# The two middle column chunks of both output projections: four of eight quads as seven products instead of eight, and the residual turned in the last chunk

## The chip, the cores and the metric

One core of one Trainium2 chip runs the whole program. The time is the device's, in microseconds (us) for one execution. A span is the time from the first to the last instruction that the profiler recorded in one profiled execution.

## What is computed

A decoder trunk of two layers on 256 tokens of width 2048, in float32. Cut to what matters:

```
for layer in (0, 1):
    h = rmsnorm(x, ln_mix_g[layer])
    x = x + mixer(h)          # its last step: o (256 x 2048) @ w_o (2048 x 2048)
    h = rmsnorm(x, ln_mlp_g[layer])
    x = x + square(relu(h @ w_up)) @ w_down     # 2048 -> 8192 -> 2048
```

The mixer of layer 0 has eight stick-breaking and eight forgetting-attention heads, that of layer 1 is latent attention with sixteen heads. Both end in an output projection of the 16 heads' outputs, 128 columns each, with `w_o` (layer 0) and `mla_w_o` (layer 1).

## The kernel before, in words

**Precision.** A float32 operand is split into a rounded high half and a low half, and each product is three matmuls: high by high, high by low, low by high. The activations' halves lie in `h` (normed residual, turned so that the width is on the partitions) and `a` (attention outputs or feed-forward activations, turned too). The weights' halves are made while they stream through.

**Pieces.** All weights pass in one fixed order of *pieces*, numbered through the kernel. SyncE loads 512 rows by 512 columns (1 MB) into one of four `raw` slots; a slot makes two pieces of 128x1024. ScalarE rounds a piece to its high half (`split_hi`, L756, copy at L769), VectorE subtracts to get the low half (`split_lo`, L1075, L1078), TensorE multiplies. There are four pairs of halves, and `AHEAD` is 4: `split_hi(n + 4)` waits until TensorE has used piece n. TensorE's piece waits for `lo_done`, VectorE's split for `hi_done`. Each engine has one queue in program order. What else an engine does behind piece n stands in a plan (`plan_steps`, L225), a list of named steps for each piece; each engine's `mixer` function (ScalarE L976, VectorE L1321, TensorE L1764) walks over the pieces and does its part of the steps.

**An output projection** is four column chunks o0 to o3 of eight pieces each. A piece covers two 128-row tiles of w_o; with two token tiles it is 4 products of 3 matmuls of 128x512, 12 matmuls (`piece_rows`, L1534). Two PSUM banks hold a chunk's sum for the two token tiles. When a chunk is done VectorE adds it to the residual `x_tok` (L1332). Three pieces into the next chunk TensorE turns the four new 128-column tiles of the residual (`turn_x`, L1610, eight transposes by the identity), ScalarE takes the squares and the high halves (`turned_x`, L811), VectorE the low halves (`h_split`, L1093); this is done in o1, o2 and o3 for the chunk before, and for the last chunk behind the third piece of the feed-forward part. In o0 the last four heads of the attention are still being computed, among the pieces.

**The feed-forward part** is four blocks a layer. A block has four up chunks (`piece_cols`, L1583; 8 matmuls of 512 columns and 8 of 256 a piece), then chunk 0 of the down projection, then chunks 1 and 2 together as a *set*, then chunk 3. The set is cut along its rows into eight *quads* (two 128-row tiles by two column chunks by two token tiles: 2x2 blocks times 2x2 blocks). A plain quad (`plain_quad`, L1851) is two pieces and 8 products. A fast quad (`fast_quad`, L1835) has 7 products (Winograd's form), in four pieces:

- the raw piece of column chunk 1 (6 matmuls), as before;
- `t13` (6 matmuls), sums of neighbouring weight blocks that POOL's DMA makes (`u_load`, `u_add`, L669 to L691): two loads of 256 KB into a `u_sum` buffer, then two more that add onto it;
- `t24` (6 matmuls), two further sums by VectorE (`weight_sums`, L1382, additions at L1391 and L1393);
- `b22` (3 matmuls), one half-size piece of 128x512.

It needs sums of the activations too: VectorE makes four of 128x128 (`token_sums`, L1395 to L1407), ScalarE rounds them (`token_sums_hi`, L1020), VectorE makes their low half (`token_sums_lo`, L1409). Six of eight quads are fast there. Their token sums are made during the up chunks and chunk 0. Eight PSUM banks X1 to X8 collect the products; at the end ScalarE copies two of them (L1049) and VectorE joins the sums in twelve `combine` steps (L1417), the last four of them the additions to the residual.

**POOL's queue** has, in mixer 0, eight products for the forget gates (L659), each waiting for a head's scores; in mixer 1 rotary products and the halves of heads 16 to 29 (`split_out`, L710); and in both feed-forward parts the weight sums (L693).

Of the kernel before, what the change touches and what calls it, by code (L numbers as in the profile page):

```python
# [57 lines left out]

def plan_chunks():

    def full(matrix, col, width=N, k_tiles=KT):
        return [(matrix, 4, 4 * P * l, col, width) for l in range(k_tiles // 4)]
# [10 lines left out]
    for c in range(4):  # L73
        first.append((f"o{c}", "cols", full("w_o", c * N)))
# [6 lines left out]
    for c in range(4):  # L81
        second.append((f"o{c}", "cols", full("mla_w_o", c * N)))
    return first, second
# [4 lines left out]
PLAIN_QUADS = 2, 5  # L88
U_BUFFER = 0, 1, 2, 3, 0, 1
BLOCK_PIECES = 32 + 8 + 4 * len(FAST_QUADS) + 2 * len(PLAIN_QUADS) + 8  # L90


P_MIX0 = 0
P_MLP0 = 2 * sum(len(c[2]) for c in MIX0)
P_MIX1 = P_MLP0 + NB * BLOCK_PIECES
P_MLP1 = P_MIX1 + 2 * sum(len(c[2]) for c in MIX1)
P_END = P_MLP1 + NB * BLOCK_PIECES
L_MLP0 = P_MLP0 // 2
L_MIX1 = L_MLP0 + 32 * NB
L_MLP1 = L_MIX1 + (P_MLP1 - P_MIX1) // 2  # L100
# [10 lines left out]
def block_no(layer, b0):  # L111
    return NB * layer + b0
# [22 lines left out]
def summed_count(layer, b0, m):  # L135

    return 32 * (3 * block_no(layer, b0) + m // 2 + 1)


def stepped_count(layer, b0, m):  # L140
    return 2 * (6 * block_no(layer, b0) + m + 1)
# [6 lines left out]
def all_pieces():  # L148
    out, seen = {}, set()

    def put(n, kind, load, half, count=0):
        out[n] = (kind, load, half, kind in ("raw", "b22") and load not in seen, count)
        if kind in ("raw", "b22"):
            seen.add(load)
    for n in range(P_MIX0, P_MLP0):
        put(n, "raw", n // 2, n % 2)
    for n in range(P_MIX1, P_MLP1):
        put(n, "raw", L_MIX1 + (n - P_MIX1) // 2, n % 2)
    for layer in range(2):
        for b0 in range(NB):  # L160
            for i, (kind, load, half) in enumerate(block_plan(layer, b0)):
                count = {"t13": summed_count(layer, b0, load), "t24": stepped_count(layer, b0, load)}.get(kind, 0)
                put(block_base(layer, b0) + i, kind, load, half, count)
    return out
# [6 lines left out]
def pieces_of(chunks, start):  # L171

    out, n = {}, start
    for _, _, loads in chunks:
        for _, kts, _, _, width in loads:
            out[n] = out[n + 1] = (kts // 2, width)
            n += 2
# [10 lines left out]
def chunk_starts(chunks, start):  # L188
    out, n = {}, start
    for name, _, loads in chunks:  # L190
        out[name] = n
        n += 2 * len(loads)
    return out


AT0, AT1 = chunk_starts(MIX0, P_MIX0), chunk_starts(MIX1, P_MIX1)


ROWS0 = {c[0]: n for n, c in enumerate(x for x in MIX0 if x[1] != "cols")}
ROWS1 = {c[0]: n + len(ROWS0) for n, c in enumerate(x for x in MIX1 if x[1] != "cols")}  # L200
# [5 lines left out]
LAST_TURN_BANK = 0, 4, 6  # L206
GAIN_COL = (0, 32, 16, 48)
# [17 lines left out]
def plan_steps():  # L225
# [75 lines left out]
    at(o + 5, ("probs", 31), ("out", 30), ("out", 31))  # L301
    for at_, chunks in ((AT0, MIX0), (AT1, MIX1)):
# [13 lines left out]
    for n in [*range(P_MIX0, P_MLP0), *range(P_MIX1, P_MLP1)]:  # L316
        if n >= FIRST - 1 and not any(what == "split" for what, _ in plan.get(n, [])):
            plan.setdefault(n, []).insert(0, ("split", 0))
    plan[AT0["k2"]].sort(key=lambda step: ("probs", "split").index(step[0]))
# [13 lines left out]
def build(nc, x, positions, ln_mix_g, ln_mlp_g, sf_w_in, sf_b_f, fox_q_g, fox_k_g, sf_w_o,  # L333
# [4 lines left out]
    with ExitStack() as ctx:  # L338
# [7 lines left out]
        x_tok = sb("x_tok", [P, TT, D])  # L346
        h = sb("h", [P, KT, 2, T], F32R)
# [90 lines left out]

        def out_on_pool(n):

            return 16 <= n < 30
# [7 lines left out]
        X1, X2, X3, X4, X5, X6, X7, X8 = (psum[:, b] for b in (2, 6, 4, 7, 0, 5, 1, 3))  # L449
# [60 lines left out]
        def raw_piece(n):  # L510
# [5 lines left out]
            if kind[0] == "t":  # L516
                pair = u_sum[U_BUFFER[load]] if kind == "t13" else v_sum[load % 2]
# [107 lines left out]
        def _(pool):  # L625
# [28 lines left out]

            pool.wait_ge(cum_ready, 1)
            for n in range(NHG):
                if n >= 2:
                    pool.wait_ge(scores_done, NHG + n - 1)
# [1288 lines left out]
```

## Time and profile before

| | us |
|---|---|
| median of 3 runs | 2058.27 (2058.08 to 2058.28) |
| the profiled execution's own time | 2057.91 |
| its span | 2056.2 |
| TensorE busy (matmuls) | 2049.1 |
| VectorE busy | 1453.8 |
| ScalarE busy | 1109.3 |
| POOL busy | 217.2 |

PE is TensorE (PEld its weight loads), DVE VectorE, ACT ScalarE, POOL GpSimd, SP SyncE. Matmuls overlap, so the duration of one (389 ns) is more than the distance from one start to the next, and a full PE row is no statement about its speed. A row of the timeline is an instruction, or several of the same line one after the other: start in us, duration in us, engine, line, operation, what it writes and reads, shape, and in brackets how long the engine was idle ahead of it and who ended that.

### The profile page before, as it was taken

The page shows a single profiled execution, that of the slowest core. Times are in us where ns is not written, and L with a number is a line of the kernel's source. Part 1 is how long each engine was busy: PE and PEld are TensorE (multiplying, and loading weights), DVE is VectorE, ACT ScalarE, POOL GpSimd, SP SyncE. Part 2 cuts the span into 40 slices and gives each one's busy share as a digit, 9 for nine tenths or more (in the row PEclk, how much of TensorE's full clock was granted, in tenths as well). Part 3 has the DMA queues.
Part 4 walks back from the last instruction along what each step waited for, and adds up shares of the span by engine and source line. Part 5 has one row for each costly group of instructions (what it writes and reads, how often), then busy time and mean ns, then how long its engine had stood idle before and what let it go on. Part 6 is the DMA issues. An engine that isn't in the chain of part 4 may idle for free.

```text
span 2056.2 us, 26460 instructions
## 1 busy us (share of the span) xinstructions
PE 2049.1 (100%) x10488; PEld 1757.1 (85%) x10488; DVE 1453.8 (71%) x1967; ACT 1109.3 (54%) x1592; POOL 217.2 (11%) x317
## 2 busy tenths in 40 slices
PE   9999999999999999999999999999999999999999
PEld 8898888888888888888889888888888888888887
DVE  6556555566966877786696788557786696687777
ACT  6555565454644544554466786444554464454454
POOL 0000000020210120110010255001110021012010
PEclk9999999999999999999999999999999999999999
DMA  8555555585885795696576533568696588679565
GB/s 286 174 154 182 170 165 163 185 252 197 258 265 195 233 289 178 201 308 204 189 244 188 157 124 122 169 203 246 198 306 202 194 260 265 200 226 291 180 199 190
DMA packets 222195, 432.35 MB, mean 210 GB/s; under 512 B 12076, under 2 KB 26488, under 8 KB 222072
## 3 DMA queue, kind: packets, MB, share of 16 engines
q1 hardware_dynamic: 200520, 380.29, 55.6%
q0 software_dynamic: 21504, 50.34, 10.6%
q8 instruction: 84, 1.38, 0.3%
q14 instruction: 39, 0.32, 0.0%
q10 hardware_dynamic: 48, 0.02, 0.0%
HBM read 428.52 MB, written 2.10 MB: 209 GB/s over the span
## 4 chain that ended last, share of the span: by engine, by line
PE 98%; ACT 1%; DVE 1%; issue 0%; POOL 0%; POOLq 0%; DVEq 0%
PE psum L1592 23%; PE psum L1545 14%; PE psum L1547 14%; PE psum L1546 14%; PE psum L1595 12%; PE psum L1829 5%; PE psum L1828 5%; PE psum L1830 5%; PE psum L1674 1%; PE psum L1761 1%; PE psum L1616 1%; PE psum L1738 0%; PE psum L1762 0%; PE psum L1718 0%; PE psum L1719 0%; ACT nat L841 0%
## 5 line engine op out<-in xcount | busy, mean ns | idle before, releaser
L1078 DVE TENSOR_TENSOR halves<-raw,halves 128x1024 fp32r<-128x1024 f32 (+2 forms) x736 | 852.9, 1166 | 442.3 <-ACT halves L769 438.2
L769 ACT CAST halves<-raw 128x1024 fp32r<-128x1024 f32 (+2 forms) x736 | 728.3, 1001 | 593.3 <-PE psum L1547 298.6
L1592 PE MATMUL psum<-h,halves 128*128 128x512 f32 x2048 | 489.8, 391 | 0.0
L1592 PEld LDWEIGHTS psum<-h,halves 128*128 128x128 f32 x2048 | 376.4, 188 | 72.8
L1545 PE MATMUL psum<-halves,a 128*128 128x512 f32 x828 | 325.4, 393 | 0.3 <-ACT mix L836 0.3
L1547 PE MATMUL psum<-halves,a 128*128 128x512 f32 x828 | 322.6, 390 | 0.0
L1546 PE MATMUL psum<-halves,a 128*128 128x512 f32 x828 | 322.2, 389 | 0.0
L1595 PEld LDWEIGHTS psum<-h,halves 128*128 128x128 f32 x2048 | 262.7, 191 | 10.0
L1595 PE MATMUL psum<-h,halves 128*128 128x256 f32 x2048 | 266.1, 283 | 0.0
L1545 PE MATMUL psum<-halves,h 128*128 128x512 f32 (+4 forms) x572 | 213.4, 373 | 0.2 <-DVE h L1276 0.2
L1547 PE MATMUL psum<-halves,h 128*128 128x512 f32 (+4 forms) x572 | 206.9, 362 | 0.0
L1546 PE MATMUL psum<-halves,h 128*128 128x512 f32 (+4 forms) x572 | 206.5, 361 | 0.0
L1547 PEld LDWEIGHTS psum<-halves,a 128*128 128x128 f32 x828 | 155.4, 188 | 32.7
L1545 PEld LDWEIGHTS psum<-halves,a 128*128 128x128 f32 x828 | 155.5, 188 | 31.9 <-ACT mix L836 0.6
L1546 PEld LDWEIGHTS psum<-halves,a 128*128 128x128 f32 x828 | 155.6, 188 | 31.5
L682 POOL DMA_DIRECT2D mix<-in_mlp_w_down x48 | 29.5, 628 | 1193.3 <-DVE halves L1078 1117.2
L1547 PEld LDWEIGHTS psum<-halves,h 128*128 128x128 f32 x572 | 107.5, 188 | 15.4
L1545 PEld LDWEIGHTS psum<-halves,h 128*128 128x128 f32 x572 | 107.7, 188 | 14.5 <-issue 0.6
L1546 PEld LDWEIGHTS psum<-halves,h 128*128 128x128 f32 x572 | 107.8, 188 | 13.9
L1828 PE MATMUL psum<-halves,a 128*128 128x512 f32 x272 | 105.8, 389 | 0.0
L1829 PE MATMUL psum<-halves,a 128*128 128x512 f32 x272 | 105.8, 389 | 0.0
L1830 PE MATMUL psum<-halves,a 128*128 128x512 f32 x272 | 105.8, 389 | 0.0
(265 smaller groups left out, 2083.8 us busy)
## 6 DMA issues: line engine op xcount, KB each, us to landing
raw<-in_mlp_w_up SPq DMA_DIRECT2D x128, 1024.0 KB, 6.1
raw<-in_mlp_w_down SPq DMA_DIRECT2D x128, 1024.0 KB, 5.2
mix<-in_mlp_w_down POOLq DMA_DIRECT2D x192, 256.0 KB, 7.1
raw<-in_sf_w_in SPq DMA_DIRECT2D x41, 1024.0 KB, 5.2
raw<-in_sf_w_o SPq DMA_DIRECT2D x16, 1024.0 KB, 5.2
raw<-in_mla_w_o SPq DMA_DIRECT2D x16, 1024.0 KB, 5.1
raw<-in_mla_w_ukv SPq DMA_DIRECT2D x8, 1024.0 KB, 5.5
raw<-in_sf_w_in SPq DMA_DIRECT2D x14, 512.0 KB, 3.9
```

The costliest lines, as they stand in the source:

```text
L682: pool.dma_start(u[:, 0], b11).then_inc(u_loaded[m % 2], 16)
L769: nc.scalar.copy(half_piece(n, 0), raw_piece(n)).then_inc(hi_done, 1)
L1078: v.tensor_tensor(half_piece(n, 1), raw_piece(n), half_piece(n, 0).bitcast(F32), ALU.subtract)\
L1545: mm(bank, x_hi, hi[:, i], start=(k == 0), stop=False)
L1546: mm(bank, x_hi, lo[:, i], start=False, stop=False)
L1547: last = mm(bank, x_lo, hi[:, i], start=False, stop=(k == total_kts - 1))
L1592: last = mm(bank, half_piece(n, 0)[:, cols], src[:, k].rearrange("p s t -> p (s t)"), start=(k == 0), stop=(k == KT - 1))
L1595: last = mm(bank[:, T:2 * T], half_piece(n, 1)[:, cols], src[:, k, 0], start=False, stop=False)
L1616: ins = nc.tensor.transpose(psum[:, bank + i // 2, col:col + P], x_tok[:, tt, k * P:(k + 1) * P], ident[:])
L1828: mm(bank, x_hi, w_hi, start=start, stop=False)
L1829: mm(bank, x_hi, w_lo, start=False, stop=False)
L1830: return mm(bank, x_lo, w_hi, start=False, stop=stop)
```

## The change

Both output projections become o0, a *set* (chunks 1 and 2 together) and o3. In the set the quads 1, 3, 5, 7 are fast, in the form of the feed-forward set, and 0, 2, 4, 6 plain: 24 pieces in place of 16. The pieces of the set are numbered 0 to 23 here: quads at 0-1, 2-5, 6-7, 8-11, 12-13, 14-17, 18-19, 20-23. The loads of the two chunks alternate on SyncE's queue. The attention outputs exist only as halves in `a`, so VectorE first adds them (`out_y`), then makes the four sums. The steps of the plan: token sums behind the seventh piece of o0 and behind set pieces 1, 7, 13, their low halves one piece later; weight sums behind the seventh piece of o0 (ahead of the split there) and behind set pieces 3, 9, 15; the twelve combination steps from set piece 22 to the fifth piece of o3; the residual's three turns behind the fourth, sixth and eighth piece of o3. The first four pieces of the feed-forward part wait for two parts of `h`. POOL gets the loads and adds of four sums in each mixer. The halves of the token sums use parts of `h`, which is free then. The feed-forward blocks keep their form and only count their semaphores on.

```diff
+def output_chunks(matrix):
+    pairs = [load for both in zip(full(matrix, N), full(matrix, 2 * N)) for load in both]
+    return [("o0", "cols", full(matrix, 0)), ("set", "set", pairs), ("o3", "cols", full(matrix, 3 * N))]
...
+OUT_FAST = 1, 3, 5, 7
+OUT_PLAIN = 0, 2, 4, 6
+OUT_SET = 4 * len(OUT_FAST) + 2 * len(OUT_PLAIN)
+OUT_U = (2, 0, 3, 1), (1, 2, 3, 0)
...
+OUT_TURN_BANK = 2, 6, 2
...
-    for o in (AT0["o0"], AT1["o0"]):
-        for c in range(3):
-            at(o + 8 * (c + 1) + 2, ("turn_x", c))
...
+    for at_ in (AT0, AT1):
+        first, start, end = at_["o0"], at_["set"], at_["o3"]
+        for i, n in enumerate((first + 6, start + 1, start + 7, start + 13)):
+            at(n, ("tokens", i))
+            at(n + 1, ("tokens_lo", i))
+        for m, n in enumerate((first + 6, start + 3, start + 9, start + 15)):
+            at(n, ("weight_sums", m))
+        at(start + out_quad(7) - 1, ("join", 3))
+        at(start + out_quad(7), ("join", 0))
+        for i, parts in enumerate(((1,), (2, 3), (4, 5), (6, 7), (8, 9), (10, 11), (12,))):
+            at(end - 2 + i, *(("combine", part) for part in parts))
+        for c in range(3):
+            at(end + 3 + 2 * c, ("turn_x", c))
...
             for n in range(NHG):
                 if n >= 2:
                     pool.wait_ge(scores_done, NHG + n - 1)
+                if n == 6:
+                    pool.wait_ge(squared, 4)
+                    out_load(0, 0)
                 pool.tensor_scalar(side_r[:, n % 2], cum_j, pick[:, n:n + 1], None, ALU.mult).then_inc(decay_ready, 1)
+            pool.wait_ge(out_done, 12)
+            out_load(0, 1)
+            out_add(0, 0)
+            out_add(0, 1)
...
-            for n in (28, 29):
-                split_out(n)
+            pool.wait_ge(out_done, 28)
+            out_load(1, 0)
+            pool.wait_ge(turned, 39)
+            out_load(1, 1)
+            split_out(28)
+            out_add(1, 0)
+            split_out(29)
+            out_add(1, 1)
+            pool.wait_ge(turned, 40)
+            out_load(1, 2)
+            pool.wait_ge(out_done, 32)
+            out_load(1, 3)
+            out_add(1, 2)
+            out_add(1, 3)
...
+            def out_tokens_hi(mixer, i):
+                made = fast_before(mixer_no(mixer)) + i
+                act.wait_ge(a_step, 4 * made + 4)
+                nc.scalar.copy(out_sd(i)[:, :, 0], out_sum).then_inc(sd_hi, 1)
...
+            def out_tokens(mixer, i):
+                made = fast_before(mixer_no(mixer)) + i
+                k0 = 2 * OUT_FAST[i]
+                if made:
+                    dve.wait_ge(sd_ready, made)
+                if i == 0:
+                    dve.wait_ge(pieces_used, AT[mixer]["o0"])
+                dve.wait_ge(out_ready, 16 * mixer + k0 + 2)
+                own(v.tensor_tensor(out_y, a[:, k0:k0 + 2, 0].bitcast(F32), a[:, k0:k0 + 2, 1].bitcast(F32), ALU.add))
+                four_sums(out_sum, out_y, made)
+
+            def out_tokens_lo(mixer, i):
+                dve.wait_ge(sd_hi, fast_before(mixer_no(mixer)) + i + 1)
+                v.tensor_tensor(out_sd(i)[:, :, 1], out_sum, out_sd(i)[:, :, 0].bitcast(F32), ALU.subtract)\
+                 .then_inc(sd_ready, 1)
...
+            def out_fast(mixer, n, q, added):
+                first, last, i = q == OUT_FAST[0], q == OUT_FAST[-1], OUT_FAST.index(q)
+                pe.wait_ge(sd_ready, fast_before(mixer_no(mixer)) + i + 1)
+                s1, s2, s3, s4 = (tuple(out_sd(i)[:, j, s] for s in range(2)) for j in range(4))
+                X1, X2, X3, X4, X5, X6, X7, _ = OUT_X
+                begun = X2, X3, X4
+                for i, parts in enumerate((((X1, tokens(2 * q, 0), 0), (X2, tokens(2 * q + 1, 0), 1)),
+                                           ((X5, s1, 0), (X7, s3, 1)),
+                                           ((X6, s2, 0), (X4, tokens(2 * q + 1, 1), 1)),
+                                           ((X3, s4, 0),))):
+                    pe.wait_ge(lo_done, n + i + 1)
+                    if first and i == 1:
+                        pe.wait_ge(x_added, added)
+                    for bank, x, half in parts:
+                        start = first and not any(bank is other for other in begun)
+                        ins = product(bank, *x, n + i, half, start, last)
+                    ins.then_inc(pieces_used, 1)
...
+            def out_steps(mixer, n, added, splits, norm):
+                for what, arg in steps_after(n):
+                    if what == "turn_x":
+                        if arg < 2:
+                            pe.wait_ge(combined, 10 * mixer_no(mixer) + (6, 3)[arg])
+                        else:
+                            pe.wait_ge(split_done, splits + 1)
+                        pe.wait_ge(x_added, added + arg)
+                        turn_x(arg, OUT_TURN_BANK[arg])
...
                         if b0 == 0 and c == 0:
-                            pe.wait_ge(split_done, splits0 - 4 + j // 2 + 1)
+                            pe.wait_ge(split_done, splits0 - 4 + max(2, j // 2 + 1))
```

## Rows read from the trace of the kernel before

**Rows 1.** The page, part 1: busy time of each engine, share of the span, instructions

```profile
PE 2049.1 (100%) x10488; PEld 1757.1 (85%) x10488; DVE 1453.8 (71%) x1967; ACT 1109.3 (54%) x1592; POOL 217.2 (11%) x317
```

**Rows 2.** Waits of TensorE: line, releaser, us in total, times, longest

```profile
PE psum L1603 <- POOL ident L635: 1.6, 1, 1.6
```

**Rows 3.** Stretches: us, then busy us (instructions) per engine, clock, DMA share, GB/s

```profile
336.00:404.00 68.00, 68.00 (x314) 56.55 (x313) 37.70 (x43) 32.96 (x49) 0.00 (x0) 1.00 0.59 186
...
512.00:552.00 40.00, 40.00 (x178) 33.14 (x177) 35.78 (x39) 25.15 (x28) 8.10 (x13) 1.00 0.81 253
```

**Rows 4.** Timeline of TensorE, first output projection, chunk o1

```profile
335.64 0.39 PE L1545 MATMUL psum<-halves,a 128*128 128x512 f32 x1
...
343.58 0.39 PE L1547 MATMUL psum<-halves,a 128*128 128x512 f32 x1
...
344.60 0.48 PE L1545 MATMUL psum<-halves,a 128*128 128x512 f32 x1
344.91 0.40 PE L1546 MATMUL psum<-halves,a 128*128 128x512 f32 x1
```

**Rows 5.** Timeline of VectorE: additions of chunks 0 and 3, first mixer

```profile
335.84 1.28 DVE L1332 TENSOR_TENSOR x_tok<-x_tok,psum 128x512 f32<-128x512 f32 x2 [0.36 <-PE psum L1547]
...
403.84 1.28 DVE L1332 TENSOR_TENSOR x_tok<-x_tok,psum 128x512 f32<-128x512 f32 x2 [0.36 <-PE psum L1547]
```

**Rows 6.** Timeline of VectorE, combination steps of a feed-forward block

```profile
558.90 0.68 DVE L1431 TENSOR_TENSOR mix<-psum,mix 128x512 f32<-128x512 f32 x1
559.50 1.22 DVE L1078 TENSOR_TENSOR halves<-raw,halves 128x1024 fp32r<-128x1024 f32 x1
```

**Rows 7.** Timeline of VectorE, feed-forward block, around and in its set

```profile
505.22 0.29 DVE L1402 TENSOR_TENSOR heads<-nat 128x128 f32<-128x128 f32 x1
...
506.15 1.22 DVE L1078 TENSOR_TENSOR halves<-raw,halves 128x1024 fp32r<-128x1024 f32 x1
507.29 0.69 DVE L1391 TENSOR_TENSOR heads<-raw,mix 128x512 f32<-128x512 f32 x1
508.01 0.69 DVE L1393 TENSOR_TENSOR heads<-raw,heads 128x512 f32<-128x512 f32 x1
...
519.38 1.23 DVE L1078 TENSOR_TENSOR halves<-mix,halves 128x1024 fp32r<-128x1024 f32 x1 [0.19 <-ACT halves L769]
...
531.14 0.69 DVE L1078 TENSOR_TENSOR halves<-raw,halves 128x512 fp32r<-128x512 f32 x1 [1.01 <-ACT halves L769]
531.75 0.69 DVE L1391 TENSOR_TENSOR heads<-raw,mix 128x512 f32<-128x512 f32 x1
```

**Rows 8.** Timeline of ScalarE, the same block

```profile
506.27 0.62 ACT L1022 CAST sd_nat<-heads 128x512 fp32r<-128x512 f32 x1 [2.18 <-DVE heads L1407]
506.80 2.00 ACT L769 CAST halves<-raw 128x1024 fp32r<-128x1024 f32 x2
...
518.30 1.05 ACT L769 CAST halves<-mix 128x1024 fp32r<-128x1024 f32 x1 [0.36 <-PE psum L1830]
...
530.48 0.62 ACT L769 CAST halves<-raw 128x512 fp32r<-128x512 f32 x1 [1.61 <-PE psum L1830]
```

**Rows 9.** Timeline of VectorE, second mixer, end of the last key product

```profile
1265.12 0.69 DVE L1231 TENSOR_TENSOR mix<-mix,st 128x512 f32<-128x512 f32 x1
```

**Rows 10.** Timeline of TensorE, the turn that waits for it

```profile
1265.87 0.66 PE L1674 MATMUL psum<-ident,mix 128*128 128x128 f32 x4 [0.31 <-DVE mix L1231]
```

**Rows 11.** Timeline of VectorE, second mixer, end of o0

```profile
1291.49 1.23 DVE L1078 TENSOR_TENSOR halves<-raw,halves 128x1024 fp32r<-128x1024 f32 x1 [0.53 <-ACT halves L769]
...
1295.62 1.28 DVE L1332 TENSOR_TENSOR x_tok<-x_tok,psum 128x512 f32<-128x512 f32 x2 [0.36 <-PE psum L1547]
```

**Rows 12.** Timeline of POOL, second mixer: end of head 27, start of head 29

```profile
1272.69 0.74 POOL L714 TENSOR_TENSOR a<-nat,a 128x256 fp32r<-128x256 f32 x1
...
1284.49 0.40 POOL L713 CAST a<-nat 128x256 fp32r<-128x256 f32 x1 [3.89 <-ACT nat L969]
```

**Rows 13.** DMA issues: queue, count, KB each, median us to landing

```profile
mix<-in_mlp_w_down POOLq DMA_DIRECT2D x192, 256.0 KB, 7.1
```

More of the change, by code:

```diff
@@ L72, in plan_chunks @@
                 first.append((f"{what}{g}", "rows", full("w_in", col)))
-    for c in range(4):
-        first.append((f"o{c}", "cols", full("w_o", c * N)))
+    first += output_chunks("w_o")
     second = [("ckva", "rows", full("w_down", RANK, CKV)),
@@ L80, in plan_chunks @@
         second.append((f"uq{g}", "rows", full("w_uq", g * 2 * QKD, 2 * QKD, 4)))
-    for c in range(4):
-        second.append((f"o{c}", "cols", full("mla_w_o", c * N)))
-    return first, second
+    return first, second + output_chunks("mla_w_o")
 MIX0, MIX1 = plan_chunks()
@@ L111, in block_no, with mixer_no, fast_before, out_quad @@
 def block_no(layer, b0):
-    return NB * layer + b0
+    return (NB + 1) * layer + 1 + b0
+def mixer_no(mixer):
+    return (NB + 1) * mixer
+def fast_before(no):
+    return sum(len(OUT_FAST if i % (NB + 1) == 0 else FAST_QUADS) for i in range(no))
+def out_quad(q):
+    return sum(4 if p in OUT_FAST else 2 for p in range(q))
 def pair_loads(layer, b0, l):
@@ L132, in block_plan, with summed_count, stepped_count, output_plan @@
     return plan + [("raw", load + j // 2, j % 2) for j in range(56, 64)]
[L135 to L141, printed above, removed]
+def summed_count(no, m):
+    return 32 * (fast_before(no) // 2 + m // 2 + 1)
+def stepped_count(no, m):
+    return 2 * (fast_before(no) + m + 1)
+def output_plan(load):
+    plan = []
+    for q in range(8):
+        one, two = load + q // 2 * 2, load + q // 2 * 2 + 1
+        plan += [("raw", one, q % 2)]
+        if q in OUT_FAST:
+            m = OUT_FAST.index(q)
+            plan += [("t13", m, 0), ("t24", m, 0), ("b22", two, q % 2)]
+        else:
+            plan += [("raw", two, q % 2)]
+    return plan
 def quad_at(q):
@@ L173, in pieces_of @@
     out, n = {}, start
[L174 to L177, printed above, removed]
+    for chunk in chunks:
+        if chunk[1] != "set":
+            for l, (_, kts, _, _, width) in enumerate(chunk[2]):
+                out[n + 2 * l] = out[n + 2 * l + 1] = (kts // 2, width)
+        n += pieces_in(chunk)
     return out
@@ L318, in plan_steps @@
             plan.setdefault(n, []).insert(0, ("split", 0))
+    for at_ in (AT0, AT1):
+        plan[at_["o0"] + 6].sort(key=lambda step: step[0] != "weight_sums")
     plan[AT0["k2"]].sort(key=lambda step: ("probs", "split").index(step[0]))
@@ L516, in raw_piece @@
             if kind[0] == "t":
-                pair = u_sum[U_BUFFER[load]] if kind == "t13" else v_sum[load % 2]
+                if kind == "t13":
+                    mixer = next((i for i, p in enumerate((P_MLP0, P_MLP1)) if AT[i]["set"] <= n < p), None)
+                    pair = u_sum[(U_BUFFER if mixer is None else OUT_U[mixer])[load]]
+                else:
+                    pair = v_sum[load % 2]
                 return pair.rearrange("p i n -> p (i n)")
@@ new lines, in out_plain @@
+            def out_plain(n, q):
+                first, last = q == OUT_PLAIN[0], q == OUT_PLAIN[-1]
+                _, X2, X3, X4, _, _, _, X8 = OUT_X
+                for i, banks in enumerate(((X2, X4), (X3, X8))):
+                    pe.wait_ge(lo_done, n + i + 1)
+                    for half in range(2):
+                        for tt in range(TT):
+                            ins = product(banks[tt], *tokens(2 * q + half, tt), n + i, half,
+                                          first and half == 0, banks[tt] is X8 and last and half == 1)
+                    ins.then_inc(pieces_used, 1)
@@ L1765, in mixer @@
                 n = start
                 for name, kind, loads in chunks:
+                    added = NORM_ADDED[norm] + 1
+                    if kind == "set":
+                        for q in range(8):
+                            if q in OUT_FAST:
+                                out_fast(mixer, n + out_quad(q), q, added)
+                            else:
+                                out_plain(n + out_quad(q), q)
+                        n += OUT_SET
+                        continue
```

221 lines of the change are left out of this document (142 added, 79 removed).

## The prediction

> **What bounds the kernel now.** I read the page first: TensorE is busy for 2049.1 of the 2056.2 us [rows 1]. The list of its waits comes next: the longest is 1.6 us, at the kernel's start [rows 2], and asked for the two stretches below the list is empty. The stretches by engine show the same: in the three chunks of the first output projection after the first (336 to 404 us) TensorE is full, VectorE busy 37.7 of 68.0 us and ScalarE 33.0, at a granted clock of 1.00; in the seven-product stretch of a feed-forward block VectorE is busy 35.8 of 40 us, and TensorE still never waits [rows 3]. So time is matmuls times their spacing, and a removed matmul pays in full unless the change makes TensorE wait. That is the question here: VectorE and ScalarE are asked for more in a stretch with fewer matmuls.
>
> **The matmuls.** The first matmul of chunk o1 starts at 335.64 and the 36th at 343.58 [rows 4], so the spacing is 7.94/35 = 0.227 us. As a check, 288 matmuls and three turns of the residual lie between the additions at 335.84 and 403.84 [rows 5]: 68.0 us. A plain quad is 8 products of 3 matmuls, a seven-product quad 21 matmuls. Four quads in each of two mixers: 24 matmuls less, 24 x 0.227 = **5.44 us gained**, if nothing waits. The Trainium skill, TensorE: Matmul & The Clock Gate, section on the back-to-back issue gap, gives about 131 ns for each of a stream of 512-column matmuls with weight loads; by that the gain would be 3.1 us. This trace shows 227 ns, and the sum goes by it.
>
> **The turns.** 24 transposes a mixer leave o1 to o3 and come in o3, the same number. One turn costs TensorE 344.60 - 343.58 less a matmul's 0.23, and the first matmul behind it is followed after 0.31 instead of 0.23 [rows 4]: 0.87 us before and after. The moved turns wait for combination steps 6 and 10 and for 12. In o3 a piece is 12 x 0.227 = 2.72 us, VectorE does two combination steps (0.6 each) [rows 6] and a split (1.14) [rows 7] in it, 2.4 us, and keeps up; the turns come three pieces or more behind what they need. VectorE's part of a turn is four operations of 256 columns, under four of the 512-column ones. The third turn ends after o3's last piece, but the first four pieces of the MLP now need only two parts of h, so it has four pieces to be ready. Cost nothing; without that cover one ScalarE and VectorE part of a turn, about 3 us a mixer.
>
> **VectorE and ScalarE in the set.** ScalarE rounds piece n+4 when TensorE has done with n, VectorE then makes its low half. Meanwhile TensorE has pieces n+1 to n+3. Back to back, VectorE needs 1.14 us for a 1024-column split, 0.61 for a 512-column one, 0.72 for a 512-column operation whose end it waits for, 0.93 for the four token sums (505.22 to 506.15) and 1.33 for a pair of weight sums (0.72 and 0.61) [rows 7]. One plain and one fast quad (six pieces, 45 matmuls, 10.2 us) ask of VectorE 5 x 1.14 + 0.61 + (0.72 + 0.93 + 0.61 tokens) + 1.33 (weights) = 9.9 us. It is enough on average, barely. But order decides.
>
> **Where it waits.** The token sums of the second to fourth fast quad stand at set pieces 1, 7 and 13, each the last piece of a plain quad. Behind that piece's end both engines work strictly in program order. ScalarE first rounds the 512-column piece (n+4); then its next instruction is the rounding of the token sums, which waits for VectorE; only behind it stands the rounding of piece n+5, the first of the next plain quad. Laid out step by step: TensorE's piece ends and the waiting engine starts 0.20 later (335.64 to 335.84) [rows 4, 5]; ScalarE's 512-column rounding to VectorE's start 0.66 (530.48 to 531.14); that split 0.61 (531.14 to 531.75); high plus low of the attention outputs, a self-waited operation, 0.72 (507.29 to 508.01); token sums 1.05 (505.22 to 506.27); ScalarE's rounding of them 0.53 (506.27 to 506.80); rounding of piece n+5 to VectorE's start 1.08 (518.30 to 519.38); its split 1.22 [rows 7, 8]. From VectorE's end to TensorE's start a row pair gives 0.06 (1265.12 + 0.69 to 1265.87) [rows 9, 10], for a transpose; that is the lower bound, three times it the upper, and I take 0.11, as two 512-column operands stand behind this wait. Sum **6.18 us**. To cover that, TensorE has pieces n+1 to n+4, one fast quad: 21 x 0.227 = 4.76 us. So it waits 1.42, and restarting costs the 0.09 seen behind a turn [rows 4]: **1.51 us**, three times in each mixer, 6 x 1.51 = **9.1 us lost**. Nothing covers it. Elsewhere in the set the same walk leaves TensorE a cover of 0.7 us or more. The feed-forward blocks don't show this wait because they make their token sums among pieces of 2.7 us and more, never inside the set. Bounds: from 1.3 (latencies of 0.05 less each) to 1.75 (VectorE late by 0.25 when the step begins) each, so 7.8 to 10.5 us together.
>
> **The first fast quad.** In the second mixer VectorE ends the split ahead of it at 1291.49 + 1.22 = 1292.7 and can add chunk 0 from 1295.62, so TensorE ended it at 1295.4 [rows 11]. From 1292.7: weight sums 1.33, split 1.14, tokens 0.72 + 0.93, chunk 0's addition 1.2, 0.5 waiting for ScalarE, split 1.14, low half 0.69: 1300.35. TensorE asks after one plain quad, at 1295.4 + 5.44 = 1300.8. Cost nothing, with 0.4 us of cover; the first mixer has the same order.
>
> **POOL and the DMAs.** Sixteen transfers of 256 KB a mixer are added. On POOL's queue they stand among the gate products (first mixer) and the splits of heads 28 and 29 (second). In the second mixer POOL is free at 1273.4, and its split of head 29 can't start before 1284.49 [rows 12]. The two loads of the first pair issue at 1273.4 and land by 1280.5, with 7.1 us a transfer [rows 13]; the adds issue near 1281 and take a microsecond, ahead of head 29, and land near 1289. VectorE comes to them at 1292.7. Cover 3.7 us, cost nothing. SP's loads keep their order of need and their slots, some 15 us ahead.
>
> **The sum.** -5.44 + 9.1 = +3.6 us. The profiled execution took 2057.91 us, 1.7 more than its span: 2056.2 + 3.6 + 1.7 = 2061.5 against it. The median is 0.36 above that execution, so 2058.27 + 3.6 = **2061.9 us**. A measurement of this kernel tells 0.2% (4.1 us) from no change: faster is under 2054.2, slower over 2062.4. The forecast is "no change", close to the upper border.
>
> **Rivals.** (1) No waits, only the gain: 2058.27 - 5.44 = 2052.8. For it: no wait in the stretch at 512 to 552 us with VectorE at 89% [rows 3]. Against it: that stretch has no token step. 6%. (2) The waits are there but about half as long, because a step of the walk overlaps or the token steps find ScalarE ahead: 3.6 - 4.5, so 2057.4 to 2060. 12%. (3) Slower: POOL's adds for the first fast quad of the second mixer land late. Transfers of 10 us instead of 7.1 end the pair at 1273.4 + 10 + 1 + 10 = 1294.4, 1.7 behind VectorE's arrival at 1292.7; less the 0.4 of cover, TensorE waits 1.3 more: 2063.2. It decides from about 0.9 us of lateness on. For it: VectorE waits there with a split queued behind. Against: the 3.7 us of cover. VectorE is also only 0.1 us ahead of the second and third token step, so slightly dearer operations end here too. 20%. (4) The granted clock falls in the waits. The trace shows 1.00 (2.4 GHz) in every stretch read, and the two stretches are there in full [rows 3]. A half clock would double the 0.227: ten matmuls at it already cost 2.3 us, so 2064 and more. 2%. The Trainium skill, TensorE: Matmul & The Clock Gate, section on a second HAM failure mode (cycling through PSUM banks), says short idles between groups can make the clock swing; by that rule this case would be likely. That the change doesn't do what it says I exclude: the new quad issues seven products in the code.
>
> **Chances.** The forecast has 60% and spans 2061.0 to 2063.0; about three tenths of it lie over 2062.4. Same: 0.42 + 0.12 = 0.54. Slower: 0.18 + 0.20 + 0.02 = 0.40. Faster 0.06. The range reaches down into rival 2 and up into rival 3: 2058.0 to 2064.5.
>
> **What would show it.** TensorE's waits should list six of about 1.5 us at the first product line of the plain quads, on VectorE's splits, none elsewhere; ScalarE six waits of about 2.5 us on the token sums; the distance from the addition of chunk 0 to that of chunk 3 should grow from 68.0 to about 69.8 us; the clock stays 1.00. A list of TensorE's waits without these makes the prediction wrong, as does a wait at the first fast quad or at the start of an MLP.

## The result, and the profile after

| | before | after |
|---|---|---|
| median, runs side by side | 2058.08 (2057.31 to 2058.64, 17 runs) | 2061.65 (2061.05 to 2062.57, 17 runs) |
| span of the profiled execution | 2056.2 | 2060.3 |

The changed kernel is slower by 3.57 us, a ratio of 1.0018 with a 95% interval of 1.0012 to 1.0025. That is inside the 0.2% that the prediction set as "no change", close to its upper border; the interval of the ratio lies above 1, so the kernel is slower, if by little. The prediction was 3.6 us and 2061.9.

The page of the kernel after, its first two lines and part 1. It answers to [rows 1]:

```profile
span 2060.3 us, 26622 instructions
## 1 busy us (share of the span) xinstructions
PE 2044.3 (99%) x10464; PEld 1750.8 (85%) x10464; DVE 1503.8 (73%) x2063; ACT 1126.9 (55%) x1620; POOL 240.2 (12%) x349
```

The 24 matmuls are gone (10488 to 10464), TensorE is busy for 4.8 us less, and the span is longer all the same. So TensorE has begun to wait. Its list of waits was led by 1.6 us at the kernel's start [rows 2]. Now (line, releaser, us in total, times, longest):

```profile
PE psum L2058 <- DVE halves L1214: 7.2, 6, 1.2
PE psum L1782 <- POOL ident L712: 1.6, 1, 1.6
```

And in the list of ScalarE's waits, the rounding of the token sums:

```profile
ACT h L1098 <- DVE h_plain L1581: 20.4, 8, 3.0
```

Six TensorE waits of 1.2 us of idle stand at one line, the first product of a plain quad. L1214 is VectorE's split, L887 ScalarE's rounding of a piece, L1472 to L1477 the addition of the halves and the low half of the token sums, L1576 to L1581 the four sums, L1098 ScalarE's rounding of them. ScalarE's eight waits include the two of the first fast quads, which delay nothing. Here is the first of the six, from the timeline of the kernel after. Of this timeline and of those below only the rows of the path are shown; most matmuls and all weight loads in between are left out. Each row is start, duration, engine, line, what is written and read, and in brackets the idle time ahead of it and what ended it:

```profile
341.54 0.39 PE L2058 MATMUL psum<-halves,a 128*128 128x512 f32 x1
341.74 0.62 ACT L887 CAST halves<-raw 128x512 fp32r<-128x512 f32 x1 [1.61 <-PE psum L2060]
342.39 0.69 DVE L1214 TENSOR_TENSOR halves<-raw,halves 128x512 fp32r<-128x512 f32 x1 [0.24 <-ACT halves L887]
343.00 0.69 DVE L1472 TENSOR_TENSOR h_plain<-a 128x512 f32<-128x512 f32 x1
343.72 0.29 DVE L1576 TENSOR_TENSOR h_plain<-h_plain 128x128 f32<-128x128 f32 x1
...
344.45 0.29 DVE L1581 TENSOR_TENSOR h_plain<-h_plain 128x128 f32<-128x128 f32 x1
344.78 0.62 ACT L1098 CAST h<-h_plain 128x512 fp32r<-128x512 f32 x1 [2.42 <-DVE h_plain L1581]
345.30 2.94 ACT L887 CAST halves<-raw 128x1024 fp32r<-128x1024 f32 x3
...
346.07 0.39 PE L2060 MATMUL psum<-halves,h 128*128 128x512 f32 x1
346.38 1.23 DVE L1214 TENSOR_TENSOR halves<-raw,halves 128x1024 fp32r<-128x1024 f32 x1 [1.64 <-ACT halves L887]
347.66 0.50 PE L2058 MATMUL psum<-halves,a 128*128 128x512 f32 x1 [1.21 <-DVE halves L1214]
348.00 0.40 PE L2059 MATMUL psum<-halves,a 128*128 128x512 f32 x1
```

Read it as one path. TensorE leaves a piece at 341.54. ScalarE rounds the half-size piece, VectorE splits it, adds the halves and makes four sums; ScalarE has stood idle for 2.42 us with its queue blocked at L1098. Only then can it round the next full piece (345.30), VectorE splits that at 346.38 after 1.64 us of idle of its own, and TensorE starts at 347.66: 6.12 us after it left the piece. It had 21 matmuls to do in that time, the last one begun at 346.07. All three engines stand still in turn.

The loss of one wait: the list above counts 1.2 us of idle, but that begins at the end of the last matmul. From the start of the last matmul to the start of the one behind the wait it is 1.59 us, the next starts 0.34 later, together 1.93 where two spacings take 0.454. So 1.48 us is lost. It happens six times (at 347.66, 359.36, 371.06 and 1309.32, 1321.02, 1332.72), together 8.9 us, against the 5.44 gained: +3.4.

The stretch from 336 to 404 us of the kernel after, by engine and with the columns of [rows 3]; then, from TensorE's timeline, its first matmul of o0 and its first of the feed-forward part:

```profile
336.00:404.00 68.00, 64.38 (x290) 52.51 (x289) 58.32 (x83) 39.03 (x54) 1.76 (x2) 1.00 0.67 205
```

```profile
306.47 0.39 PE L1724 MATMUL psum<-halves,a 128*128 128x512 f32 x1
...
405.77 0.48 PE L1771 MATMUL psum<-h,halves 128*128 128x512 f32 x1
```

VectorE went from 37.70 to 58.32 us of 68, TensorE lost 3.62 us of them (three waits of 1.2 us), and the clock stayed at 1.00. Before, these two matmuls stood at 306.02 and 403.64 in TensorE's timeline: the section has grown from 97.62 to 99.30 us, by 1.68. Three waits less half the gain is 3 x 1.48 - 2.72 = 1.72. The second mixer gives the same three waits. A wait of 0.25 us near 1290 (at head 31) and 0.45 us at the kernel's start make up what is left of the span's 4.1 us. The start is scatter: in the ten profiled executions of this record, whose TensorE does the same work up to there, the first matmul of o0 stands anywhere between 305.76 and 306.47 us.

### The profile page after: what moved, and what is told of

The parts are those of the page before. It is cut to its first block, busy times and chain, and to the rows that moved or that the text cites. A ratio compares the mean times of both kernels' runs of the same rounds, so it can differ in the third digit from the quotient of the medians.

```text
span 2060.3 us, 26622 instructions
## 1 busy us (share of the span) xinstructions
PE 2044.3 (99%) x10464; PEld 1750.8 (85%) x10464; DVE 1503.8 (73%) x2063; ACT 1126.9 (55%) x1620; POOL 240.2 (12%) x349
## 4 chain that ended last, share of the span: by engine, by line
PE 95%; DVE 3%; ACT 1%; issue 1%; DMA 0%; SPq 0%; ACTq 0%; DVEq 0%
PE psum L1771 23%; PE psum L1724 13%; PE psum L1726 13%; PE psum L1725 13%; PE psum L1774 12%; PE psum L2058 6%; PE psum L2060 6%; PE psum L2059 6%; DVE halves L1214 2%; PE psum L1853 1%; PE psum L1940 1%; ACT halves L887 1%; PE psum L1795 1%; PE psum L1917 0%; PE psum L1941 0%
## 5 line engine op out<-in xcount | busy, mean ns | idle before, releaser
L1214 DVE TENSOR_TENSOR halves<-raw,halves 128x1024 fp32r<-128x1024 f32 (+2 forms) x736 | 848.5, 1160 | 400.6 <-ACT halves L887 396.7
L887 ACT CAST halves<-raw 128x1024 fp32r<-128x1024 f32 (+2 forms) x736 | 723.3, 996 | 550.2 <-PE psum L1726 249.2
L1724 PE MATMUL psum<-halves,a 128*128 128x512 f32 x700 | 275.4, 393 | 0.3 <-ACT mix L954 0.3
L1726 PE MATMUL psum<-halves,a 128*128 128x512 f32 x700 | 272.8, 390 | 0.0
L1725 PE MATMUL psum<-halves,a 128*128 128x512 f32 x700 | 272.4, 389 | 0.0
L1726 PEld LDWEIGHTS psum<-halves,a 128*128 128x128 f32 x700 | 131.4, 188 | 27.8
L1724 PEld LDWEIGHTS psum<-halves,a 128*128 128x128 f32 x700 | 131.5, 188 | 27.0 <-ACT mix L954 0.7
L1725 PEld LDWEIGHTS psum<-halves,a 128*128 128x128 f32 x700 | 131.5, 188 | 26.5
L2058 PE MATMUL psum<-halves,a 128*128 128x512 f32 x360 | 140.7, 391 | 7.2 <-DVE halves L1214 7.2
L2059 PE MATMUL psum<-halves,a 128*128 128x512 f32 x360 | 140.1, 389 | 0.0
L2060 PE MATMUL psum<-halves,a 128*128 128x512 f32 x360 | 140.1, 389 | 0.0
```

Of the source, the lines that this page charges most:

```text
L887: nc.scalar.copy(half_piece(n, 0), raw_piece(n)).then_inc(hi_done, 1)
L1214: v.tensor_tensor(half_piece(n, 1), raw_piece(n), half_piece(n, 0).bitcast(F32), ALU.subtract)\
L1724: mm(bank, x_hi, hi[:, i], start=(k == 0), stop=False)
L1725: mm(bank, x_hi, lo[:, i], start=False, stop=False)
L1726: last = mm(bank, x_lo, hi[:, i], start=False, stop=(k == total_kts - 1))
L2058: mm(bank, x_hi, w_hi, start=start, stop=False)
```

## The experiments

Three theories stood before them. **The order**, theory 1: each of the six waits comes from ScalarE being blocked behind the token sums, and goes when ScalarE takes the next piece's rounding first. **The load**, theory 2: VectorE, busy for 58 of 68 us, has too much to do, and would be late in any order. **The transfers**, theory 3: POOL's sixteen further loads and additions hold up the pieces. Experiments 1 to 4 ran beside runs of the kernel before that gave 2057.89, experiments 5 to 8 beside 2058.00.

**1. The order alone.** ScalarE's rounding of the token sums of the second to fourth fast quad moves one step of its plan back, so it stands behind the rounding of piece n+5. Nothing else changes.

```diff
                             elif what == "tokens":
-                                out_tokens_hi(mixer, arg)
+                                if arg == 0:
+                                    out_tokens_hi(mixer, arg)
+                            elif what == "tokens_lo":
+                                if arg:
+                                    out_tokens_hi(mixer, arg)
```

> One change in ScalarE's order against the changed kernel: for the second to fourth fast quad it rounds the token sums one step later, behind the rounding of the next plain quad's first piece (n+5). VectorE's and TensorE's instructions, the transfers and all amounts of work stay. Theory 1 (order on ScalarE): VectorE then gets piece n+5 rounded while it still makes the token sums, so from the end of piece n to the split's end it is 0.20 + 0.66 + 0.61 + 0.72 + 0.93 + 1.22 + 0.11 = 4.45 us against 4.76 us of matmuls: the six waits of 1.47 us go, 2061.65 - 8.8 = 2052.8 us, below the kernel before by 0.26%. Theory 2 (VectorE has too much to do in the set as a whole): the same work, so the same waits, 2061.6 us. Theory 3 (POOL's transfers and the weight sums that wait for them): unchanged too, 2061.6 us.

Measured: 2052.56 (2052.25 to 2052.87, 9 runs), ratio to the kernel before 0.9974 [0.9964, 0.9984]. All six waits are gone, in both mixers. The same stretch by engine, and the same step in the timeline of this kernel (its L1476, L1585 and L1218 are L1472, L1581 and L1214 of the kernel after, L2062 is L2058):

```profile
336.00:404.00 68.00, 68.00 (x320) 56.78 (x319) 61.33 (x87) 43.38 (x64) 1.74 (x2) 1.00 0.69 213
```

```profile
340.84 0.39 PE L2062 MATMUL psum<-halves,a 128*128 128x512 f32 x1
341.04 0.62 ACT L887 CAST halves<-raw 128x512 fp32r<-128x512 f32 x1 [1.61 <-PE psum L2064]
...
342.31 0.69 DVE L1476 TENSOR_TENSOR h_plain<-a 128x512 f32<-128x512 f32 x1
...
342.46 1.05 ACT L887 CAST halves<-raw 128x1024 fp32r<-128x1024 f32 x1 [0.79 <-PE psum L2064]
...
343.97 1.22 DVE L1218 TENSOR_TENSOR halves<-raw,halves 128x1024 fp32r<-128x1024 f32 x1
...
344.08 0.62 ACT L1098 CAST h<-h_plain 128x512 fp32r<-128x512 f32 x1 [0.57 <-DVE h_plain L1585]
...
345.60 0.39 PE L2062 MATMUL psum<-halves,a 128*128 128x512 f32 x1
```

ScalarE rounds the full piece at 342.46, while VectorE works at the sums, and VectorE's split begins at 343.97 without idle, 3.13 us behind the start of the path instead of 4.84. It ends 0.5 us before TensorE asks at 345.60. VectorE is busier in this stretch than in the kernel after (61.33 us), the transfers are all there, and TensorE is full. So theories 2 and 3 fall as causes of these waits. The version beats both kernels: 5.3 us less than before, 9.1 less than after, with the same arithmetic.

**2. The work alone.** The order of the kernel after, but the addition, the four sums, their rounding and low half are done for one column only in quads two to four. The rest of these sums is left out. Of the edit only ScalarE's rounding is shown; VectorE's operations are cut in the same way.

```diff
-                nc.scalar.copy(out_sd(i)[:, :, 0], out_sum).then_inc(sd_hi, 1)
+                cols = slice(0, 1 if i else P)
+                nc.scalar.copy(out_sd(i)[:, :, 0, cols], out_sum[:, :, cols]).then_inc(sd_hi, 1)
```

> The changed kernel with the token sums of the second to fourth fast quad cut to one column of 128 (the addition of the halves, the four sums, the rounding and the low half), so these three quads of each mixer multiply sums that were not made; order and number of instructions stay. Theory 1: the chain behind piece n falls by the width of the operations, 0.6 + 0.6 + 0.4 us, to about 4.6 us, under the 4.76 us of matmuls: no wait, 2052.8 us. Theory 2: VectorE loses some 12 us of work, 2052.8 us as well. Theory 3: the weight sums and transfers are all still there, 2061.6 us.

Measured: 2053.14 (2052.75 to 2053.62, 10 runs), ratio 0.9977 [0.9968, 0.9986], no waits there. VectorE's timeline of this kernel at the same step:

```profile
341.92 0.69 DVE L1215 TENSOR_TENSOR halves<-raw,halves 128x512 fp32r<-128x512 f32 x1 [0.24 <-ACT halves L887]
342.53 0.15 DVE L1474 TENSOR_TENSOR h_plain<-a 128x2 f32<-128x2 f32 x1
...
343.11 0.16 DVE L1586 TENSOR_TENSOR h_plain<-h_plain 128x1 f32<-128x1 f32 x1
344.48 1.22 DVE L1215 TENSOR_TENSOR halves<-raw,halves 128x1024 fp32r<-128x1024 f32 x1 [1.22 <-ACT halves L887]
```

VectorE still waits 1.22 us for ScalarE, so the blocked order is still there; the path is only short enough. Shortening the path cures TensorE's wait as reordering it does. This kernel alone could not tell order from load, since it takes load away and shortens the path at once.

**3. A dose on the path.** The addition of the halves is made twice in the six steps.

```diff
-                own(v.tensor_tensor(out_y, a[:, k0:k0 + 2, 0].bitcast(F32), a[:, k0:k0 + 2, 1].bitcast(F32), ALU.add))
+                for _ in range(2 if i else 1):
+                    own(v.tensor_tensor(out_y, a[:, k0:k0 + 2, 0].bitcast(F32), a[:, k0:k0 + 2, 1].bitcast(F32), ALU.add))
```

> The changed kernel with the addition of the two halves made twice in the second to fourth token step of each mixer, 0.72 us more of VectorE each time. Theory 1: it stands on the path in front of ScalarE's rounding, so each of the six waits grows by 0.72 us to about 1.9 us of idle time: 2061.65 + 4.3 = 2066.0 us. Theory 2: if only VectorE's sum of work counted, the 0.1 us by which it is ahead would be used up first and the growth would be a little less, 2065.3 us. Theory 3: no change, 2061.6 us.

Measured: 2071.24 (2069.77 to 2072.41, 4 runs), ratio 1.0065 [1.0051, 1.0079]: 9.6 us more than the kernel after, over twice the 4.3 expected. The waits did what was expected, 0.72 each (1.59 to 2.31 us from start to start). The excess is in the stretches behind them (same columns as above, the clock is the third number from the end):

```profile
347.00:350.00 3.00, 2.25 (x8) 1.77 (x9) 3.00 (x4) 2.27 (x3) 0.00 (x0) 0.83 0.18 72
350.00:353.00 3.00, 3.00 (x10) 2.40 (x9) 2.97 (x4) 0.35 (x1) 0.00 (x0) 0.60 0.01 3
353.00:356.00 3.00, 3.00 (x15) 2.47 (x14) 1.43 (x3) 1.32 (x2) 0.00 (x0) 1.00 1.00 315
```

```profile
347.75 0.51 PE L2059 MATMUL psum<-halves,a 128*128 128x512 f32 x1 [1.92 <-DVE halves L1214]
348.09 0.40 PE L2060 MATMUL psum<-halves,a 128*128 128x512 f32 x1
...
349.08 0.63 PE L2061 MATMUL psum<-halves,a 128*128 128x512 f32 x1
349.51 0.63 PE L2059 MATMUL psum<-halves,a 128*128 128x512 f32 x1
...
352.07 0.53 PE L2059 MATMUL psum<-halves,a 128*128 128x512 f32 x1
```

Behind the wait of 1.92 us five matmuls run at the usual spacing, then seven spacings from 349.08 to 352.07 are 0.43 us: the granted clock is 0.50 in the stretch from 349.3 to 352.0 us, its lower level, 1.2 GHz. TensorE is "busy" all the time, with 10 matmuls in 3 us instead of 13. It happened behind four of the six waits, for 7 or 8 matmuls each; 12.4 us for 29 spacings that would take 6.6 is 5.8 us. The spacings at either end of these stretches, partly slowed (0.28 to 0.37 us), add 0.6. With 4.3 for the waits that is 10.7, against 10.6 of this profiled execution (2072.22).

**4. The turns alone.** The kernel before, with only the residual's turns of chunks o0 to o2 moved behind the fourth, sixth and eighth piece of o3, with the waits and PSUM banks that go with them (of the edit the move alone is shown).

```diff
-            at(o + 8 * (c + 1) + 2, ("turn_x", c))
+            at(o + 24 + 3 + 2 * c, ("turn_x", c))
```

> The kernel before with one part of the change alone: the three turns of the residual moved from o1, o2 and o3 to behind the fourth, sixth and eighth piece of o3, and the first pieces of the feed-forward part waiting for two parts of h. No fast quads. Forecast: the turns cost the same 0.87 us wherever they stand and nothing waits for them: 2058.1 us, within 0.5. Rival: the third turn comes late for the feed-forward part or the moved turns wait for the additions, up to 3 us a mixer, 2061 to 2064 us.

Measured: 2058.00 (2057.64 to 2058.17, 11 runs), ratio 1.0000 [0.9991, 1.0009]. The moved turns cost nothing.

**5. The dose of experiment 3 in the mended order.** Both edits (1 and 3) together.

> The doubled addition of the third experiment (0.72 us more VectorE work in each of six token steps; the result is the same) put into the version whose order is mended. Order theory: the 0.72 now lies in VectorE's queue alone, ahead of the split of piece n+5, and no longer in a walk that goes through ScalarE and back. The mended version's walk ends some 0.3 us ahead of TensorE, so about 0.3 to 0.45 of each 0.72 comes through, six times, with a restart of 0.09 where TensorE waits: 2052.6 + 6 x 0.54 = 2055.8, and no stretch at a low clock, since no wait is longer than about 0.5 us. Rival, the cover is wide once the order is right (a further 0.7 us or more): 2052.6. Rival, the dose itself and not the wait brings the clock down: about 2060 as in the third experiment less its waits, with matmuls 0.43 us apart.

Measured: 2055.97 (2055.59 to 2056.69, 10 runs), ratio 0.9990 [0.9981, 1.0000]: 3.4 us over the mended version. TensorE's waits:

```profile
PE psum L2063 <- DVE halves L1218: 1.2, 6, 0.2
```

Six short ones, 0.59 + 0.33 us between starts where two spacings take 0.45: 0.47 us each, 2.8 in all, the rest mostly at the kernel's start. The same 0.72 us of VectorE work costs 0.72 and the low clock in the one order, and 0.47 and no low clock in the other. The late start is 0.59 - 0.23 = 0.36 us of the 0.72, so the cover of the mended order is some 0.4 us.

**6. A dose behind the weight sums, mended order.** One more addition of 128x512, whose result nothing reads, behind each pair of weight sums of quads two to four.

```diff
                 half_sums(one, q % 2, u_sum[OUT_U[mixer][m]], no, m)
+                if m:
+                    own(v.tensor_tensor(out_y, a[:, 0:2, 0].bitcast(F32), a[:, 0:2, 1].bitcast(F32), ALU.add))
```

> One addition of 128x512 (0.72 us, into a tile that is not read again before it is overwritten) behind each pair of weight sums of the second to fourth seven-product quad, in the version whose order is mended. In a set of 45 matmuls (10.2 us) VectorE was counted at 9.9 us, so it has 0.3 us to give. Load theory: 0.4 us of it come through at each of the token steps behind the second and third dose, in both mixers: 2052.6 + 4 x 0.3 + 0.1 = 2053.9. Rival, the count of 9.9 is too high and nothing comes through: 2052.6. Rival, it is too low and most of each comes through: 2052.6 + 6 x 0.72 = 2056.9.

Measured: 2053.78 (2053.45 to 2054.29, 10 runs), ratio 0.9979 [0.9970, 0.9989]. Against the first experiment 1.2 us more, where 1.2 and 0.1 were expected. In the profiled executions (1.6 us apart) it is made up otherwise: in each mixer 0.36 us are lost at the fourth fast quad's token step (366.88 and 1324.62) and 0.15 at the third's (356.29 and 1314.02), not 0.3 at both, and 0.45 lie at the kernel's start. So the total agrees in part by luck: the first dose is all but absorbed, and of the second half comes through.

**7. The same dose in the kernel after's own order.**

> The same three additions behind the weight sums, but in the changed kernel with its own order. Tests the step by which VectorE is only 0.1 us ahead of the second and third token step: if so, the dose makes it late there, and four of the six waits grow by 0.6 while the first of each mixer stays: 2061.7 + 4 x 0.6 = 2064.1. Rival, VectorE has more than 0.7 us of slack there and the waits stay as they are: 2061.7. Added to either: where an idle of TensorE grows to 1.7 us or more its granted clock may fall as in the third experiment, some eight matmuls at 0.43 instead of 0.23 us, 1.5 us for each such wait: up to 2070.

Measured: 2066.75 (2065.37 to 2066.89, 5 runs), ratio 1.0040 [1.0026, 1.0054]. From start to start the six waits are 1.59, 2.17, 1.59 and 1.60, 2.21, 2.20 us. The first of each mixer has no dose ahead and is unchanged; three of the other four grew by 0.6, as expected. The exception is the third, and the clock explains it. Behind the second wait it fell, TensorE was slower, and VectorE made up its lateness: ahead of the third token step it stood idle for 0.91 us, which it did ahead of no other dosed step. In the second mixer the clock did not fall behind the second wait, and the third grew. The windows (columns as above), then VectorE's split ahead of the third token step:

```profile
360.00:363.00 3.00, 3.00 (x9) 2.30 (x9) 2.96 (x5) 1.28 (x2) 0.00 (x0) 0.55 0.00 0
...
1324.00:1327.00 3.00, 3.00 (x15) 2.44 (x14) 2.96 (x5) 1.41 (x3) 0.00 (x0) 1.00 0.00 0
...
1337.00:1340.00 3.00, 3.00 (x9) 2.35 (x8) 2.93 (x5) 0.49 (x1) 0.00 (x0) 0.52 0.02 5
```

```profile
367.80 0.69 DVE L1214 TENSOR_TENSOR halves<-raw,halves 128x512 fp32r<-128x512 f32 x1 [0.91 <-ACT halves L887]
```

Three waits 0.6 longer are 1.8 us. Two low stretches, each of 8 spacings in 3.39 us instead of 1.81, are 3.2. Together 2061.65 + 5.0 = 2066.7. The three waits grew by 0.58 to 0.62 for a dose of 0.72, so VectorE had 0.10 to 0.14 us of slack ahead of these steps.

**8. A half dose on the path.** In the kernel after, half of the addition (128x256) is made once more in the six steps.

```diff
+                if i:
+                    own(v.tensor_tensor(out_y[:, 0], a[:, k0, 0].bitcast(F32), a[:, k0, 1].bitcast(F32), ALU.add))
```

> In the changed kernel, half of the addition of the halves (128x256) is made once more in each of the six token steps, so the idle of TensorE lies between the changed kernel's 1.2 us, where every matmul ran at the full clock, and the third experiment's 1.9, where four of six waits were followed by seven or eight matmuls 0.43 us apart. Order theory for the waits: each grows by about 0.42, 2061.7 + 6 x 0.42 = 2064.2. Clock, if an idle of 1.6 us is enough as well: 1.5 us more for each wait that is followed by the low clock, up to 2070 for four. Clock, if it is not: 2064.2, and no two matmuls of the set 0.43 us apart.

Measured: 2064.75 (2064.11 to 2065.72, 5 runs), ratio 1.0033 [1.0019, 1.0046]. The waits are 2.04 us from start to start, 0.45 more each, 2.7 in all, and behind none of them did a matmul run at 0.43:

```profile
347.00:350.00 3.00, 2.60 (x11) 2.15 (x12) 2.96 (x5) 1.94 (x3) 0.00 (x0) 1.00 0.06 25
350.00:353.00 3.00, 3.00 (x14) 2.47 (x14) 3.00 (x4) 1.06 (x1) 0.00 (x0) 1.00 0.17 22
```

## Why the prediction was right, point by point

- **The matmuls**, -5.44 at 0.227 us each: confirmed by the mended version, which has all of the change and none of the waits. It is 2057.89 - 2052.56 = 5.33 us faster than before. The 131 ns of the Trainium skill (TensorE: Matmul & The Clock Gate, section on the back-to-back issue gap) would have made the gain 3.1; the trace decides.
- **The walk**, 6.18 us against 4.76: the trace after has 6.12 from 341.54 to 347.66, and 0.34 instead of 0.31 for the restart. The loss is 1.48 each where 1.51 was put, 8.9 for the six instead of 9.1. Its steps came out within 0.01 (0.20, 0.65, 0.61, 0.72, 1.06, 0.52, 1.08); the last split with the start of TensorE behind it took 1.28 instead of 1.33 (the 1.22 put for the split is its shown duration; VectorE's next instruction starts 1.14 behind it, so the hand-over was 0.14 and not 0.11). The six waits stand at the line, on the releaser and in the number named. Moving ScalarE's blocked step back (experiment 1) and lengthening the path (3 and 8) move them as the walk says, so the cause is shown and not only argued.
- **The sum**: that 3.6 predicted meets 3.57 measured so closely is in part luck. The gain and the six waits give 3.4; the profiled execution of the kernel after holds another 0.25 us at head 31, which no term of the prediction has, and the kernel's start alone scatters by 0.7 us.
- **The turns**: nothing, as predicted (experiment 4).
- **The first fast quad**: the low half of its sums was predicted at 1300.35 and TensorE's request at 1300.8, in the clock of the profile before. After, the split ahead of it stands 2.35 later (1293.84 instead of 1291.49) [rows 11]; the low half ends at 1302.6 and TensorE starts at 1303.19, with 0.6 us of cover instead of 0.4 and no wait. VectorE's and TensorE's timelines:

```profile
1293.84 1.23 DVE L1214 TENSOR_TENSOR halves<-raw,halves 128x1024 fp32r<-128x1024 f32 x1 [0.52 <-ACT halves L887]
1294.98 0.68 DVE L1561 TENSOR_TENSOR heads<-raw,mix 128x512 f32<-128x512 f32 x1
...
1299.12 1.28 DVE L1491 TENSOR_TENSOR x_tok<-x_tok,psum 128x512 f32<-128x512 f32 x2
...
1301.99 0.68 DVE L1477 TENSOR_TENSOR h<-h_plain,h 128x512 fp32r<-128x512 f32 x1
```

```profile
1303.19 0.39 PE L2058 MATMUL psum<-halves,a 128*128 128x512 f32 x1
```

- **POOL and the DMAs**: cost nothing, as predicted, but the cover was put too wide. The additions were issued as one pair, in POOL's timeline:

```profile
1283.38 1.92 POOL L755 DMA_DIRECT2D mix<-in_mla_w_o  x2 [0.51 <-DMA mix<-in_mla_w_o]
```

 The second mixer stands 2.3 us later than in the profile before, and these steps with it. They landed at 1288.14 and 1292.24, the second 8.3 us after its issue, where 7.1 and a microsecond between them were reckoned. VectorE takes the weight sums at 1294.98, without idle. The cover was 2.7 us, not 3.7. With the 0.6 us of cover behind it, the third rival (late additions) was some 3.3 us away (an estimate; no run delayed them).
- **Slack ahead of the token steps**, 0.1 us: confirmed. In the trace after, VectorE's splits follow each other 1.14 us apart, and the one ahead of the second token step starts 1.23 behind the one before it, so VectorE was idle for 0.09 us:

```profile
352.86 1.22 DVE L1214 TENSOR_TENSOR halves<-heads,halves 128x1024 fp32r<-128x1024 f32 x1
354.09 0.69 DVE L1214 TENSOR_TENSOR halves<-raw,halves 128x512 fp32r<-128x512 f32 x1
```

 In experiment 7 VectorE absorbed 0.10 to 0.14 us of each dose that came through. So the order makes the six waits, and only 0.1 us further on the load would add to them.
- **A marker that failed.** The distance between the additions of chunk 0 and chunk 3 was to grow from 68.0 to 69.8 us; it is 67.84 (337.46 to 405.30). The sum was not wrong but the marker was: both additions moved against TensorE. Chunk 0's stands on VectorE behind the weight sums and token sums now, 30.99 us behind the first matmul of o0 instead of 29.82, so 1.17 later. Chunk 3's stands ahead of the third turn now, 0.47 us ahead of the first matmul of the feed-forward part instead of 0.20 behind it, so 0.67 earlier. From TensorE's matmuls the section grew by 1.68, against 1.81 predicted, and 1.68 - 1.17 - 0.67 = -0.16 is the marker's change. Both moves stand in the prediction's own paragraphs (chunk 0's addition after the tokens; the third turn after o3's last piece).
- **The clock**, rival 4: not in the changed kernel, where it was 1.00 in all 17 runs, but much nearer than a chance of 2% says. Waits 0.6 us longer bring it (experiment 7), and then one fall costs 1.6 us; the rival put 2.3 for ten matmuls, and the falls seen held 7 or 8.

## What to carry to other kernels

Before moving a step into a software pipeline, lay its path out across the engines' queues: a helper operation that waits for another engine, put ahead of the rounding of the next piece, makes three engines stand still in turn, with ScalarE at 57% and VectorE at 86% load. Issue first what the bottleneck needs next, and the instruction that waits for another engine behind it; here that one move, at three steps of each mixer, turned +3.6 us into -5.3. To test such a theory, move the blocked instruction alone and keep the work: taking the work away cannot tell order from load.

## What the runs showed of the hardware

The granted clock fell behind short single waits. Ahead of each of these waits stand matmuls at the full clock and the usual spacing, and behind it TensorE has its full work again. They came out so (one profiled execution of each kernel):

| start to start across the wait, us | idle in the list, us | waits | followed by matmuls 0.43 us apart |
|---|---|---|---|
| 1.59 (kernel after; experiment 7) | 1.2 | 6; 3 | 0; 0 |
| 2.04 (experiment 8) | 1.7 | 6 | 0 |
| 2.17 to 2.21 (experiment 7) | 1.8 | 3 | 2 |
| 2.31 (experiment 3) | 1.9 | 6 | 4 |

Each fall came two to five matmuls after TensorE had started again, to the lower level (1.2 GHz), and cost 1.6 us with the partly slowed spacings at its ends. The wait ahead of it cost 2.1 to 2.2. The Trainium skill, TensorE: Matmul & The Clock Gate, section on a second HAM failure mode, says that frequent micro-idles can make the clock swing and lower the throughput. The runs with idles of 1.8 us and more agree, those with 1.2 and 1.7 us do not. Why some waits of one length are followed by it and others not stays open. The number of falls changes between executions of one kernel: the mean clock of a run tells it. The profiled execution of experiment 3, with four falls, has a mean of 0.996, that of experiment 7, with two, 0.998. The other runs of experiment 3 have 0.996 (2072.41 us), 0.997 (2070.27) and 0.998 (2069.77), the fastest of experiment 7 has 0.999 (2065.37), 1.4 us under the median at 0.998. All 17 runs of the kernel after and all five of experiment 8 have 1.000 (the means are rounded to three places, and one fall takes about 0.001 off), so their waits of 1.2 and 1.7 us were followed by no fall in any of them.
